# Six modulation chunks of the second layer: products and sums on GpSimd in place of TensorE

## The chip, the cores and the metric

The kernel runs on one core of a Trainium2 chip. The metric is device time in microseconds (us) for one execution; lower is better. Engines are named as the profile names them: PE (TensorE), PEld (TensorE's weight load), DVE (VectorE), ACT (ScalarE), POOL (GpSimd) and SP (SyncE, which here only issues transfers).

## The reference

Two blocks follow one another. The first is a transformer of two layers (256 tokens, width 2048) with three kinds of attention. The second is a block with retention, an mLSTM and a mixture of experts, and its norms are modulated by six rows that come from one vector `c`:

```
sh1, sc1, gt1, sh2, sc2, gt2 = split(silu(c) @ w_ada + b_ada, 6)
csh1, csc1, ... = split(silu(c_ctx) @ w_ada + b_ada, 6)
rq, rk, ... = split_in(modulate(x, norm1_g, sh1, sc1) @ w_in)
crq, ...    = split_in(modulate(ctx, norm1_g, csh1, csc1) @ w_in)
x = x + gt1 * merge(...)
x = x + gt2 * peer(modulate(x, norm2_g, sh2, sc2), ...)
```

`w_ada` is 2048 x 12288. Of the rows for the context only `csh1` and `csc1` are used, since the context isn't updated in the last (here the only) layer.

## The kernel before

All large weights come through one ring of four buffers, `ring`, each 128 x 2048 numbers (1 MB, a "piece"): SP issues one transfer after the other (L882), in the order of the list `RING`, each after a wait on `piece_used` of its buffer. A weight piece is then cut into a high part by ACT (the cast to `high`, L1883) and a low part by DVE (the subtraction `ring_r`, L2506). PE multiplies it in three passes (L300 to L302), 24 matmuls of 512 columns for a piece, and its last matmul counts `piece_used` up, whereupon SP may fill the buffer anew. Inside a layer the pieces have slots 0 to 87; beside the slots PE does the attention's matmuls.

`w_ada` is cut into 24 chunks of 512 columns. Fourteen are done within the two layers: chunk `a` has four pieces that stand in the ring between weight pieces, after the slots of `ADA_SLOTS` (seven chunks for each layer). These modulation pieces are not split. For each, PE runs `ada_pe` (L340): four fp32 matmuls with two stationary columns (silu of `c` and of `c_ctx`) and 512 moving columns, one in each quarter of the array, into PSUM bank 7. After the fourth piece ACT copies the four quarters' rows to `mod_rows` in SBUF (`ada_act`, L359), PE sums them over the quarters and turns them into columns (`ada_turn`, L353), and DVE copies these into `adac` (`ada_dve`, L368). Other work in this stretch that the change stands beside: POOL issues side transfers in a written order (query weights, the residual, context columns, `pT` and `w_ple` for the embedding products at L1245), each after a wait for the slot that frees its place.

Of the kernel before, what the change touches and what calls it, by code (L numbers as in the profile page):

```python
# [26 lines left out]
ALU = mybir.AluOpType  # L27
# [3 lines left out]
P = 128  # L31
# [4 lines left out]
PIECE_KT = 4  # L36
CHUNK = 512
PIECE = PIECE_KT * CHUNK
PIECES = 4
DEPTH = 2  # L40
# [77 lines left out]
C_SILU = C_CONV + 3 * 8  # L118
# [17 lines left out]
ADA_SLOTS = ((3, 5, 7, 9), (12, 14, 16, 18), (28, 30, 32, 34), (38, 40, 42, 44), (59, 61, 63, 65), (68, 70, 72, 74), (77, 79, 81, 83))  # L136
ADA_LAYER = len(ADA_SLOTS)
ADA_L = DEPTH * ADA_LAYER


def layer_order():
# [23 lines left out]
def build_program(nc, t):  # L165
    ctx = ExitStack()
    with ctx:
# [172 lines left out]
        def ada_pe(pe, a, j):  # L340
# [9 lines left out]
                               ring[:, b, q * CHUNK:(q + 1) * CHUNK], start=(j == 0), stop=(j == 3), tile_position=(0, 32 * q))  # L350
            mm.then_inc(piece_used[b], 1)

        def ada_turn(pe, a):  # L353
            pe.wait_ge(ada_rows, a + 1)
            for b in range(4):
                mm = pe.matmul(ps[:, 7, 2 * b:2 * b + 2], mod_rows[:, b * P:(b + 1) * P], sel16[:, 0:2], start=True, stop=True)
            mm.then_inc(ada_turned, 1)
# [9 lines left out]

        def ada_dve(dve, a):  # L368
            dve.wait_ge(ada_turned, a + 1)
            dve.tensor_copy(adac[:, 4 * a:4 * a + 4, :], ps[:, 7, 0:8].rearrange("p (b r) -> p b r", r=2)).then_inc(ada_done, 1)  # L370


# [579 lines left out]
        def _(pool):  # L952
            for n, (name, l) in enumerate(STAGES):
# [8 lines left out]
                elif name == "layers":  # L962
                    for l in range(DEPTH):
                        pool.wait_ge(tile_low, TILES(l, "x", 8))
                        pool.wait_ge(x_square, l + 1)
                        if l >= 1:
                            pool.wait_ge(h_spilled, 16)
                        for k in range(3):
                            if k:
                                b, u, _ = W_AT[l, 2 * k]  # L970
                                pool.wait_ge(piece_used[b], u + 1)
                            pool.dma_start(w_uq[:, k, :], t["w_uq"][l][k * P:(k + 1) * P, :]).then_inc(layer_loads, 16)
                        b, u, _ = W_AT[l, 6]
                        pool.wait_ge(piece_used[b], u + 1)
                        pool.dma_start(w_ukv, t["w_ukv"][l].rearrange("(k p) n -> p k n", p=P)).then_inc(layer_loads, 16)
                        pool.wait_ge(at_out, HEADS * (l + 1))
                        pool.wait_ge(at_done, HEADS * (l + 1))
                        pool.dma_start(hx_of[l], (HRES if l else t["x"]).rearrange("(t p) d -> p t d", p=P)).then_inc(layer_loads, 16)
                        if l + 1 == DEPTH:
                            pool.dma_start(trig[:, :, :, :], t["trig2"]).then_inc(consts_p, 16)  # L980
                            pool.dma_start(b_ada, t["b_ada"]).then_inc(consts_p, 16)
                            for e in range(4):
                                b, u, _ = W_AT[l, (57, 59, 61, 63)[e]]
                                pool.wait_ge(piece_used[b], u + 1)
                                pool.dma_start(crows[:, :, e, :], t["ctx"][:, e * CHUNK:(e + 1) * CHUNK].rearrange("(t p) d -> p t d", p=P)).then_inc(consts_p, 16)
                            pool.wait_ge(tile_full, TILES(l, "mixed", 9))
                            pool.dma_start(final_g, t["final_g"].partition_broadcast(P)).then_inc(aux, 16)
                        b, u, _ = W_AT[l, OUT_SLOT + OUT_PIECES.index((3, 1))]
                        pool.wait_ge(piece_used[b], u + 1)
                        pool.dma_start(pT, t["pT"][l].rearrange("(k p) n -> p k n", p=P)).then_inc(ple_loaded, 16)  # L990
                        for e in range(4):
                            cs = slice(e * CHUNK, (e + 1) * CHUNK)
                            if e:
                                b, u, _ = W_AT[l, (71, 73, 76)[e - 1]]
                                pool.wait_ge(piece_used[b], u + 1)
                                pool.wait_ge(ple_loaded, 80 * l + 16 * (e + 1))
                            pool.dma_start(w_ple[:, :, cs], t["w_ple"][l][:, cs].rearrange("(k p) n -> p k n", p=P)).then_inc(ple_loaded, 16)
                        if l + 1 < DEPTH:
                            pool.wait_ge(gate_used, 4 * (l + 1))
                            pool.dma_start(HRES.rearrange("(t p) d -> p t d", p=P), hx).then_inc(h_spilled, 16)  # L1000
                    for e in range(4):
                        if e == 3:
                            pool.wait_ge(ada_turned, ADA_L)
                            pool.dma_start(wgates, t["wgates"]).then_inc(aux, 16)
                        pool.wait_ge(gate_used, 4 * (DEPTH - 1) + e + 1)
                        pool.dma_start(HX[:, e * CHUNK:(e + 1) * CHUNK].rearrange("(t p) d -> p t d", p=P), hx_1[:, :, e * CHUNK:(e + 1) * CHUNK]).then_inc(h_saved, 16)
# [59 lines left out]
        def _(pe):  # L1066
# [3 lines left out]
            for n, (name, l) in enumerate(STAGES):  # L1070
                begin(pe, n, () if name in FLOWING or name == "peer" else ALL)
                if name == "layers":
# [306 lines left out]
                    for l in range(DEPTH):  # L1379
                        for q in range(SLOTS):  # L1380
                            if l == 0 and q == 3:
                                pe.wait_ge(tile_low, TILES(0, "x", 8))
                            for p, blocks in parts_of(q):
                                products(l, p, blocks)
                            if l == 0 and q < 2:
                                turn_first_x(2 + q)
                            if l:
                                side(l - 1, q + SLOTS)
                            side(l, q)
                            for a0, slots in enumerate(ADA_SLOTS):  # L1390
                                a = ADA_LAYER * l + a0
                                if q in slots:
                                    if q == 28:
                                        pe.wait_ge(rel_made, 6 * (l + 1))
                                    elif q == 59:
                                        pe.wait_ge(tile_low, TILES(l, "mixed", 5))
                                    ada_pe(pe, a, slots.index(q))
                                elif q == slots[-1] + 1:
                                    ada_turn(pe, a)
                elif name == "kv":  # L1400
# [474 lines left out]
        def _(sc):  # L1875
            for n, (name, l) in enumerate(STAGES):
                begin(sc, n, () if name in FLOWING else ALL)
                if name == "layers":
# [133 lines left out]
                    def side(l, q):  # L2012
# [108 lines left out]
                            elif q - 2 in C_TURN_AT:  # L2121
                                high_of_ctx(C_TURN_AT.index(q - 2))
                        for a0, slots in enumerate(ADA_SLOTS):
                            if q == slots[-1] + 2:
                                ada_act(sc, ADA_LAYER * l + a0)

                    sc.activation(rs[:, 90:91], ones[:, 0:1], ACT.Silu)
# [354 lines left out]
        def _(dve):  # L2482
# [12 lines left out]
            for n, (name, l) in enumerate(STAGES):  # L2495
# [5 lines left out]
                elif name == "layers":  # L2501
# [457 lines left out]
                    use_gate(DEPTH - 1, 3)  # L2959
                    split_dve(dve, kv_piece(2), (2,))  # L2960
                    k0, k1 = 2 * KT, 4 * ADA_L
                    dve.tensor_tensor(adac[:, k0:k1, :], adac[:, k0:k1, :], b_ada[:, k0:k1].unsqueeze(2).to_broadcast([P, k1 - k0, 2]), ALU.add)
                    for rows in part_rows:
                        dve.memset(rows, 0.0)
                    dve.wait_ge(x_square, DEPTH + 2)
# [739 lines left out]
```

## Time and profile before

| | |
|---|---|
| median of 3 runs | 3759.24 us (3757.33 to 3761.44) |
| profiled execution | 3757.12 us, of which the span is 3755.6 us |
| PE busy | 3706.6 us, 99% of the span |
| DVE, ACT, POOL busy | 2365.3, 1575.0, 114.8 us |
| second layer with the six chunks | about 705 to 1256 us of the span |

"Busy" is the union of the instruction times of an engine. A row of the timeline gives start and duration in us, the engine, the line of the kernel, and in brackets how long the engine was idle before and what ended that.

### The profile page before, as it was taken

The numbers are of one execution on the slowest core, as the hardware profiler recorded it, in microseconds if no ns is written. First come the engines' busy times: TensorE is split into PE (matmuls) and PEld (weight loads), VectorE is DVE, ScalarE is ACT, GpSimd is POOL, SyncE is SP. The second block draws the span as 40 slices with busy tenths as digits, with TensorE's granted clock in tenths as the row PEclk, the third lists the DMA queues.
The fourth block names the chain that finished last, engine by engine and source line by source line (L and its number), as shares of the span: only waits on it lengthen the run. The fifth ranks groups of instructions, "written<-read, shape, count | busy, mean of one in ns | idle before, by whom it ended". The sixth has DMA issues, their size and how long they took to land.

```text
span 3755.6 us, 48176 instructions
## 1 busy us (share of the span) xinstructions
PE 3706.6 (99%) x20154; PEld 3123.8 (83%) x20154; DVE 2365.3 (63%) x3164; ACT 1575.0 (42%) x1562; POOL 114.8 (3%) x157
## 2 busy tenths in 40 slices
PE   8999999999999999999999999999999999999998
PEld 6777777777777778988888899999988888888886
DVE  4366545347645667565746579777566666667777
ACT  5344544344444522256443433355433333333333
POOL 0000000000000000020000000000000000000000
PEclk9999999999999999999999999999999999999999
DMA  7445565645566467543466445556666666666664
GB/s 274 168 172 202 194 262 198 269 146 191 198 261 241 161 247 283 206 173 134 153 225 246 165 172 187 207 218 229 226 236 235 223 223 223 223 246 235 236 250 175
DMA packets 119530, 799.35 MB, mean 213 GB/s; under 512 B 13424, under 2 KB 13808, under 8 KB 32304
## 3 DMA queue, kind: packets, MB, share of 16 engines
q1 hardware_dynamic: 96992, 692.73, 51.1%
q0 software_dynamic: 20048, 82.96, 5.7%
q10 hardware_dynamic: 2304, 20.97, 1.3%
q8 instruction: 142, 2.33, 0.2%
q14 instruction: 44, 0.36, 0.0%
HBM read 752.57 MB, written 44.04 MB: 212 GB/s over the span
## 4 chain that ended last, share of the span: by engine, by line
PE 93%; DVE 3%; DMA 2%; ACT 1%; POOL 1%; issue 0%; DVEq 0%; SPq 0%; POOLq 0%; ACTq 0%
PE ps L300 25%; PE ps L301 24%; PE ps L302 24%; PE ps L1808 5%; PE ps L1810 2%; DMA ring<-in_stream_dram 2%; PE ps L1760 2%; PE ps L349 1%; PE ps L1245 1%; PE ps L1109 1%; DVE ring_r L2506 1%; PE ps L1599 1%; DVE ring_r L314 1%; PE ps L1076 0%; PE ps L1077 0%; ACT high L1883 0%
## 5 line engine op out<-in xcount | busy, mean ns | idle before, releaser
L308 ACT CAST high<-ring 128x2048 fp32r<-128x2048 f32 x384 | 733.7, 1912 | 1185.0 <-DMA ring<-in_stream_dram 1180.1
L314 DVE TENSOR_TENSOR ring_r<-ring,high 128x2048 fp32r<-128x2048 f32 x384 | 880.4, 2294 | 536.9 <-ACT high L308 534.5
L302 PE MATMUL ps<-high,act_r 128*128 128x512 f32 x1952 | 762.7, 391 | 0.0
L300 PE MATMUL ps<-high,z_r 128*128 128x512 f32 x1728 | 677.8, 392 | 2.7 <-DVE ring_r L2506 2.3
L301 PE MATMUL ps<-ring_r,z_r 128*128 128x512 f32 x1728 | 673.1, 390 | 0.0
L300 PE MATMUL ps<-high,h_r 128*128 128x512 f32 x1600 | 644.9, 403 | 9.5 <-DVE ring_r L2506 5.5
L301 PE MATMUL ps<-ring_r,h_r 128*128 128x512 f32 x1600 | 625.0, 391 | 0.0
L2506 DVE TENSOR_TENSOR ring_r<-ring,high 128x2048 fp32r<-128x2048 f32 x176 | 402.9, 2290 | 348.7 <-ACT high L1883 347.2
L302 PE MATMUL ps<-high,z_r 128*128 128x512 f32 x1376 | 535.9, 389 | 0.0
L301 PE MATMUL ps<-act_r,high 128*128 128x256 f32 x1664 | 471.6, 283 | 0.0
L1883 ACT CAST high<-ring 128x2048 fp32r<-128x2048 f32 x176 | 335.0, 1909 | 252.2 <-DMA ring<-in_stream_dram 251.2
L302 PEld LDWEIGHTS ps<-high,act_r 128*128 128x128 f32 x1952 | 367.3, 188 | 79.3
L300 PE MATMUL ps<-act_r,high 128*128 128x256 f32 x1472 | 420.6, 286 | 2.4 <-DVE act_r L3388 2.4
L302 PE MATMUL ps<-act_r,ring_r 128*128 128x256 f32 x1472 | 417.3, 283 | 0.0
L300 PEld LDWEIGHTS ps<-high,h_r 128*128 128x128 f32 x1600 | 301.2, 188 | 114.9 <-issue 44.9
L300 PEld LDWEIGHTS ps<-high,z_r 128*128 128x128 f32 x1728 | 324.6, 188 | 84.0 <-issue 12.6
L301 PEld LDWEIGHTS ps<-ring_r,z_r 128*128 128x128 f32 x1728 | 324.8, 188 | 66.5 <-issue 0.5
L301 PEld LDWEIGHTS ps<-ring_r,h_r 128*128 128x128 f32 x1600 | 301.6, 189 | 58.3 <-issue 0.7
L301 PEld LDWEIGHTS ps<-act_r,high 128*128 128x128 f32 x1664 | 320.3, 192 | 0.0
L302 PEld LDWEIGHTS ps<-high,z_r 128*128 128x128 f32 x1376 | 258.3, 188 | 54.2
L1808 PE MATMUL ps<-act_r,high 128*128 128x512 f32 x832 | 294.8, 398 | 0.0
L300 PEld LDWEIGHTS ps<-act_r,high 128*128 128x128 f32 x1472 | 283.3, 192 | 2.5 <-issue 2.5
(511 smaller groups left out, 3973.8 us busy)
## 6 DMA issues: line engine op xcount, KB each, us to landing
ring<-in_stream_dram SPq DMA_DIRECT2D x656, 1024.0 KB, 4.8
hidden<-z POOLq DMA_DIRECT2D x32, 512.0 KB, 6.4
gate_matrix<-z ACTq DMA_DIRECT2D x8, 2048.0 KB, 7.2
r<-gate_matrix POOLq DMA_DIRECT2D x32, 512.0 KB, 6.2
z<-hidden POOLq DMA_DIRECT2D x32, 512.0 KB, 6.6
r<-in_w_ple_dram POOLq DMA_DIRECT2D x8, 512.0 KB, 5.8
merge_gates<-r ACTq DMA_DIRECT2D x8, 512.0 KB, 4.8
r<-merge_gates POOLq DMA_DIRECT2D x4, 1024.0 KB, 5.4
```

The source lines that it names most:

```text
L300: pe.matmul(out, lhs[0], rhs[0], start=start, stop=False)
L301: pe.matmul(out, lhs[0], rhs[1], start=False, stop=False)
L302: return pe.matmul(out, lhs[1], rhs[0], start=False, stop=stop)
L308: sc.copy(high[:, j, :], ring[:, j, :]).then_inc(piece_high[j], 1)
L314: dve.tensor_tensor(ring_r[:, j, :], ring[:, j, :], high[:, j, :], ALU.subtract).then_inc(piece_low[j], 1)
L349: mm = pe.matmul(ps[32 * q:32 * q + 2, 7, :], cols[:, C_SILU + 2 * k:C_SILU + 2 * k + 2], ring[:, b, q * CHUNK:(q + 1) * CHUNK], start=(j ...
L1109: mm = pe.matmul(ps[:, bank, (hd % 2) * TOK:(hd % 2 + 1) * TOK], w[:, k, hd * HD:(hd + 1) * HD], src[:, k, :], start=(k == 0), stop=(k == ...
L1760: mm = pe.matmul(ps[:, 4 + t // 4 % 4, (t % 4) * P:(t % 4 + 1) * P], hot1[:, k % HOTS, t % 8, :], hot2[:, k % HOTS, t % 8, :], start=True, ...
L1808: mm = pe.matmul(ps[:, b, :].rearrange("p (s n) -> p s n", s=2), w[0], halves_2(k), start=(k == 0), stop=(k == KT - 1))
L1810: mm = pe.matmul(ps[:, b, TOK:], w[1], high_2(k), start=False, stop=False)
L1883: sc.copy(high[:, b, :], ring[:, b, :]).then_inc(piece_high[b], 1)
L2506: dve.tensor_tensor(ring_r[:, b, :], ring[:, b, :], high[:, b, :], ALU.subtract).then_inc(piece_low[b], 1)
```

## The change

Chunks 8 to 13, all of which belong to the second layer and none of which the context needs, leave PE's matmuls. For each piece of these chunks POOL multiplies each of four 512-column parts by one column of silu(c) (a number for each partition) and adds it to `mod_rows`, in place, one instruction after the other with a semaphore between. POOL frees the ring's buffer when it is through the piece. PE then sums over all 128 partitions: `ada_turn` multiplies `mod_rows` by a column of ones. ACT's copies for these chunks are gone, DVE copies one column where it copied two. The pieces' places in the ring stay. In the diff `chain` is a semaphore count with a wait for it on the same engine.

```diff
+ADA_POOL = (8, 9, 10, 11, 12, 13)
...
+        def ada_pool(pool, a, j):
+            b, u = A_AT[a, j]
+            if j == 0:
+                pool.wait_ge(ada_turned, a)
+            pool.wait_ge(piece_full[b], 16 * (u + 1))
+            for q in range(PIECE_KT):
+                k = PIECE_KT * j + q
+                w, c = ring[:, b, q * CHUNK:(q + 1) * CHUNK], cols[:, C_SILU + 2 * k:C_SILU + 2 * k + 1]
+                if k == 0:
+                    o = pool.tensor_scalar(mod_rows, w, c, None, ALU.mult)
+                else:
+                    chain(pool, "pool", pool.tensor_scalar(w, w, c, None, ALU.mult))
+                    o = pool.tensor_tensor(mod_rows, mod_rows, w, ALU.add)
+                if q < PIECE_KT - 1:
+                    chain(pool, "pool", o)
+            o.then_inc(piece_used[b], 1)
+            pool.wait_ge(piece_used[b], u + 1)
+            if j == 3:
+                pool.drain().then_inc(ada_rows, 1)
...
         def ada_turn(pe, a):
             pe.wait_ge(ada_rows, a + 1)
+            if a in ADA_POOL:
+                pe.wait_ge(ada_done, a)
+                for b in range(4):
+                    mm = pe.matmul(ps[:, 7, 2 * b:2 * b + 1], mod_rows[:, b * P:(b + 1) * P], ones[:, 0:1], start=True, stop=True)
+                mm.then_inc(ada_turned, 1)
+                return
...
                         pool.dma_start(w_ukv, t["w_ukv"][l].rearrange("(k p) n -> p k n", p=P)).then_inc(layer_loads, 16)
+                        if l + 1 == DEPTH:
+                            for a in (8, 9, 10):
+                                for j in range(4):
+                                    ada_pool(pool, a, j)
...
                                 pool.dma_start(crows[:, :, e, :], t["ctx"][:, e * CHUNK:(e + 1) * CHUNK].rearrange("(t p) d -> p t d", p=P)).then_inc(consts_p, 16)
+                                ada_pool(pool, 11, e)
...
+                            ada_pool(pool, 12, 0)
+                            ada_pool(pool, 12, 1)
...
+                                if l + 1 == DEPTH and e < 3:
+                                    ada_pool(pool, 12, e + 1)
+                                elif l + 1 == DEPTH:
+                                    ada_pool(pool, 13, 0)
...
+                    for j in range(1, 4):
+                        ada_pool(pool, 13, j)
...
-                                    ada_pe(pe, a, slots.index(q))
+                                    if a not in ADA_POOL:
+                                        ada_pe(pe, a, slots.index(q))
```

On PE, at the third piece of chunk 11 (slot 63 of the second layer), `ps` is PSUM, `z_r` and `r_r` the left operands in two parts; before:

```order
L300 MATMUL ps<-high,z_r 128x512
L301 MATMUL ps<-ring_r,z_r 128x512
L302 MATMUL ps<-high,z_r 128x512
L349 MATMUL ps<-ring,cols 2x512 [waits piece_full2]
L349 MATMUL ps<-ring,cols 2x512 x3
L300 MATMUL ps<-high,r_r 128x512 [waits piece_low3,evac0]
L301 MATMUL ps<-ring_r,r_r 128x512
```

With the change the two rows of L349 are gone there, and 23 times more; the wait for `piece_low3` follows directly on slot 63's last matmul. On POOL, at the same stretch (the context's columns, the final weights' row, then chunk 12), before:

```order
L981 DMA r<-in_b_ada_dram 128x96
L985 DMA act<-in_ctx_dram 128x2x512 x4
L987 DMA z<-in_final_g_dram 128x2048
L990 DMA r<-in_pT_dram 128x2x256
L997 DMA r<-in_w_ple_dram 128x2x512 x4
```

and with the change, from the second of the four context transfers on, through the second piece of chunk 11 to the third transfer:

```order
L1020 DMA act<-in_ctx_dram 128x2x512
L366 TENSOR_SCALAR ring<-ring,cols 128x512
L367 TENSOR_TENSOR wsmall<-wsmall,ring 128x512
L366 TENSOR_SCALAR ring<-ring,cols 128x512
L367 TENSOR_TENSOR wsmall<-wsmall,ring 128x512
L366 TENSOR_SCALAR ring<-ring,cols 128x512
L367 TENSOR_TENSOR wsmall<-wsmall,ring 128x512
L366 TENSOR_SCALAR ring<-ring,cols 128x512
L367 TENSOR_TENSOR wsmall<-wsmall,ring 128x512
L1020 DMA act<-in_ctx_dram 128x2x512
```

`wsmall` holds `mod_rows`. POOL's queue now holds eight instructions (seven for the first piece of a chunk) between such transfers, each piece behind a wait for its landing.

## Rows read from the trace of the kernel before

**Rows 1.** The page: busy time (share) xinstructions; granted clock by slices, tenths.

```profile
PE 3706.6 (99%) x20154; PEld 3123.8 (83%) x20154; DVE 2365.3 (63%) x3164; ACT 1575.0 (42%) x1562; POOL 114.8 (3%) x157
PEclk9999999999999999999999999999999999999999
```

**Rows 2.** Waits of PEld from 705 to 1256 us: total, times, longest.

```profile
PEld ps L300 <- DVE ring_r L2506: 7.0, 7, 2.1
```

**Rows 3.** Busy time from 705 to 1256 us: all engines; L349 alone; L2506 alone.

```profile
705.00:1256.00 551.00, 547.06 (x2639) 424.09 (x2637) 306.06 (x506) 255.86 (x334) 10.18 (x15) 1.00 0.57 210
705.00:1256.00 551.00, 26.01 (x200) 2.66 (x200) 1.00 0.57 210
705.00:1256.00 551.00, 173.97 (x76) 1.00 0.57 210
```

**Rows 4.** Timeline: third piece of chunk 11, its buffer's next filling, that piece's way.

```profile
1094.62 0.33 SPq L882 DMA_DIRECT2D ring<-in_stream_dram  x1
1106.68 1.04 PE L349 MATMUL ps<-ring,cols 128*2 128x512 f32 x8
1107.78 0.33 SPq L882 DMA_DIRECT2D ring<-in_stream_dram  x1
1118.31 1.91 ACT L1883 CAST high<-ring 128x2048 fp32r<-128x2048 f32 x1 [2.62 <-DMA ring<-in_stream_dram]
1120.25 2.29 DVE L2506 TENSOR_TENSOR ring_r<-ring,high 128x2048 fp32r<-128x2048 f32 x1 [3.73 <-ACT high L1883]
1122.60 0.50 PE L300 MATMUL ps<-high,z_r 128*128 128x512 f32 x1 [1.16 <-DVE ring_r L2506]
```

**Rows 5.** Timeline of SP: issue and next filling, shortest (chunk 12) and longest (chunk 8).

```profile
1154.05 0.33 SPq L882 DMA_DIRECT2D ring<-in_stream_dram  x1
1167.14 0.33 SPq L882 DMA_DIRECT2D ring<-in_stream_dram  x1
743.42 0.33 SPq L882 DMA_DIRECT2D ring<-in_stream_dram  x1
774.62 0.33 SPq L882 DMA_DIRECT2D ring<-in_stream_dram  x1
```

**Rows 6.** The ring's 101 transfers of that stretch.

```profile
DMA to landing us min/median/max: 4.6/4.8/10.5
```

**Rows 7.** Timeline of POOL's twelve sums, first to last, and of DVE beside them.

```profile
1633.44 2.31 POOL L385 TENSOR_TENSOR act<-z,trig 128x512 f32<-128x512 f32 x1
...
1642.31 1.29 POOL L388 TENSOR_TENSOR act<-z,trig 128x512 f32<-128x512 f32 x1
1643.67 1.29 POOL L389 TENSOR_TENSOR z<-act 128x512 f32<-128x512 f32 x1
1644.91 3.36 POOL L390 TENSOR_TENSOR z<-act 128x512 f32<-128x512 f32 x1
...
1656.82 1.26 POOL L390 TENSOR_TENSOR z<-z 128x512 f32<-128x512 f32 x1
1632.30 5.60 DVE L314 TENSOR_TENSOR ring_r<-ring,high 128x2048 fp32r<-128x2048 f32 x2
...
1644.59 2.52 DVE L314 TENSOR_TENSOR ring_r<-ring,high 128x2048 fp32r<-128x2048 f32 x1
```

**Rows 8.** POOL's other one-tensor instructions: count, busy us, mean ns.

```profile
L957 POOL TENSOR_SCALAR_AFFINE_SELECT ident<-ident 128x128 f32<-128x128 f32 x1 | 0.3, 292 | 0.2 <-POOL ident L956 0.2
L960 POOL IOTA iota<- 128x128 f32 x1 | 0.2, 238 | 0.0
L956 POOL MEMSET ident<- 128x128 f32 x1 | 0.2, 205 | 0.3 <-POOLq L3696 0.3
L3696 POOL MEMSET const-float32-0.0<- 128x1 f32 x1 | 0.1, 98 | 0.5 <-issue 0.5
```

**Rows 9.** A side transfer of POOL, and PE's first use of what it brings.

```profile
1148.68 0.72 POOL L997 DMA_DIRECT2D r<-in_w_ple_dram  x1
...
L1245 PE MATMUL ps<-r x32: 590/592/593, 1178.9 to 1249.8; 128*128 128x512 f32 x32
```

More of the change, by code:

```diff
@@ L369, in ada_dve @@
             dve.wait_ge(ada_turned, a + 1)
+            if a in ADA_POOL:
+                dve.tensor_copy(adac[:, 4 * a:4 * a + 4, 0], ps[:, 7, 0:8:2]).then_inc(ada_done, 1)
+                return
             dve.tensor_copy(adac[:, 4 * a:4 * a + 4, :], ps[:, 7, 0:8].rearrange("p (b r) -> p b r", r=2)).then_inc(ada_done, 1)
@@ L2123, in side @@
                         for a0, slots in enumerate(ADA_SLOTS):
-                            if q == slots[-1] + 2:
+                            if q == slots[-1] + 2 and ADA_LAYER * l + a0 not in ADA_POOL:
                                 ada_act(sc, ADA_LAYER * l + a0)
@@ L2961, in _ @@
                     k0, k1 = 2 * KT, 4 * ADA_L
-                    dve.tensor_tensor(adac[:, k0:k1, :], adac[:, k0:k1, :], b_ada[:, k0:k1].unsqueeze(2).to_broadcast([P, k1 - k0, 2]), ALU.add)
+                    dve.tensor_tensor(adac[:, k0:k1, 0], adac[:, k0:k1, 0], b_ada[:, k0:k1], ALU.add)
                     for rows in part_rows:
```

## The prediction, on record before the change was timed

> **What bounds the kernel now.** I read the page first: PE is busy 99% of the span and its granted clock stays in the top tenth throughout [rows 1]; that is the 2.4 GHz level, so no clock effect is to be had. A matmul taken off PE is therefore worth its time, as long as the pieces behind it are ready earlier too. Next I cut out the stretch of the six chunks, 705 to 1256 us: PE busy 547.06 of 551 us, DVE 306.06, POOL only 10.18 [rows 3]. Then the waits: PE's loads waited seven times, 7.0 us in all, for DVE's subtraction of a ring piece [rows 2]. So in seven places the ring and not PE set the pace already. The timeline of one such place shows the chain [rows 4]: the third piece of chunk 11 is issued at 1094.62, PE multiplies it at 1106.68 for 1.04 us, its buffer is filled anew from 1107.78, that transfer lands at 1118.31 (the cast waited for it), cast and subtraction take until 1122.54, and PE, idle for 1.16 us, starts at 1122.60. Whoever frees this buffer 1 us later stops PE 1 us longer.
>
> **Taken away.** L349's rows in the stretch are 200 for 26.01 us, that is 25 pieces (one belongs to chunk 7) of 1.04 us [rows 3]. 24 go: **-25.0 us of PE**. ACT loses 24 copies of small rows and DVE half a column copy; neither was waited for at those places, so 0. `ada_turn` keeps four small matmuls: 0.
>
> **Added: POOL's time for a piece.** Four products and four sums (three for the first piece of a chunk, 3.75 on average). A sum of 128x512 alone takes 1.29 us, and after a semaphore the next starts 0.07 us later [rows 7]. There is no product in the trace. The nearest rows are one-tensor instructions of 128 columns, 205, 238 and 292 ns against 98 ns for one column [rows 8]; stretched to 512 columns they give 0.52, 0.66 and 0.87 us. I take the middle, 0.66; above, 1.29 bounds it (a sum, which reads two tensors). So 4 x 0.66 + 3.75 x 1.29 + 7 x 0.07 = 8.0 us if nothing disturbs.
>
> Something does. Of the twelve sums of 1633 us, those that met DVE's subtraction took 2.31 and 3.36 us, each ending 1.3 us after the subtraction did; the twelve took 24.6 us from first to last in place of 15.5. The subtractions were lengthened too: 5.60 us for two, 2.52 for one, against 2.29 [rows 4, 7]. The two engines shut each other out for whole instructions. The Trainium skill says just this ("SBUF — State Buffer", on what contends): a DVE instruction with two SBUF inputs and a GpSimd one that reads SBUF share a port, and the second to start blocks until the first has ended. By that rule, the trace agrees.
>
> In the stretch the subtractions alone fill 173.97 of 551 us, 32% [rows 3]: 8.0 / 0.68 = 11.8. I take **11.5 us for a piece** (low 7.4, all products at 0.52 and never blocked; high 16.6, products at 1.29 and the 1.6-fold stretching of rows 7). For the product the skill has a figure ("GPSIMD Engine Reference", performance versus the Vector engine): 0.77 us for 512 elements in a good loop. By it a piece would take an estimated 12 us and the sum below would be some 5 us worse.
>
> **Where it lands.** What counts is when the buffer is freed. Before, a piece stayed in its buffer from issue to the next filling between 13.1 us and 31.2 us (the first two rows and the last two of [rows 5]). POOL needs 4.8 us for the landing [rows 6] plus 11.5: 16.3. I went through all 24: ten stay less than 16.3 us now (three pieces each of chunks 9 and 12, three of 11, one of 10; 13.0 to 15.7, together 144.5), and these are freed later, by 18.5 us together: **+18.5**. The other fourteen are freed at the same time or earlier, which the next pieces hardly need. With 9.5 us for a piece it is three pieces and 2.9 us, with 14 us fifteen pieces and 46.6 us: this term is steep, and the forecast hangs on it.
>
> **DVE behind POOL.** POOL is busy 24 x 11.5 = 276 us, half of the stretch. Half of the 76 subtractions meet it and wait about 0.5 us (0.23 and 1.0 shown, [rows 7]): 19 us, of which PE feels what finds no slack. A third, I choose, since about a quarter of the weight pieces are ready under 1.2 us before PE takes them and the attention's DVE steps run into POOL as well: **+6**. Bounds 0 and 19.
>
> **Ring already late.** At seven places PE waited for the chain [rows 2]; the microsecond saved before them is worth something only if the chain moves too. Seven times half of 1.04: **+3.5** (0 to 7).
>
> **Moved on POOL's queue.** The transfers behind the sums: `pT` and the first `w_ple` go out at 1148.68 and are wanted at 1178.9 [rows 9]. With the second piece of chunk 12 ahead of them (issued 1141, landed 1146, 11.5 us) they go out at about 1158, so 20 us of cover is left; a POOL piece of over 20 us would spend it. The residual's saves after chunk 13 have no reader near. Cost 0. PE's turn of a chunk comes one slot after its last piece, about 7 us behind PE's old use of it, and 14 us or more behind the landing in every chunk: 0.
>
> Sum: -25.0 + 18.5 + 6 + 3.5 = **+3.0 us**. The profiled execution took 3757.12 us, which gives 3760; it lies 2.1 below the median of the runs shown, so against that median 3762. I say **3761 us**. A measurement of this kernel tells about 0.2% (7.5 us) from no change.
>
> **Rivals.**
> 1. *The sums fit.* A piece on POOL takes about 9.5 us: products at 0.52 to 0.6, and POOL slips between the subtractions. For it: POOL was idle for 540 of 551 us. Against it: the blocking of rows 7. Then -25.0 + 2.9 + 5 + 3.5 = -14, 3743 to 3750. Chance 0.27.
> 2. *POOL is the ring's slowest user.* A product costs nearer 1 us or more, or small DVE steps with two inputs each let one POOL instruction pass: 14 us a piece. Then -25.0 + 46.6, less what slack of up to 4 us for a piece takes (about half of it, 15 pieces x 1.5), + 8 + 3.5 = +10, and with 16 us some +30: 3767 to 3790. Its place is the index and selection part (chunk 9) and the output slots (chunks 11, 12), and it decides from about 12.5 us a piece. Chance 0.31.
> 3. *No effect at all*, since PE waits for the ring in place of multiplying; it lies in the forecast's range.
>
> The forecast, losses and gains nearly even (3752 to 3766), has 0.42. From these cases: faster 0.28, same 0.40, slower 0.32. Eight in ten: 3744 to 3780; the likeliest case alone 3753 to 3767.
>
> **What the profile after would show.** L349 with 256 rows in place of 448; POOL busy about 280 us more; one product 0.6 to 0.9 us; sums of 1.3 us alone and 2.3 to 3.4 beside a subtraction; subtractions above 2.29 on average; PE's waits for L2506 risen from 7 us to 25 or 30 in the stretch, after the pieces of chunks 9, 11 and 12. I am wrong if a piece takes under 10 us or over 13, if the waits of PE come from POOL's turn (`ada_rows`) or the embedding's weights, or if DVE's attention steps and not the ring stop PE.

## The result and the profile after: 0.7% slower

The changed kernel takes 3783.47 us (median of 4 runs, 3782.11 to 3787.58) where the kernel before takes 3759.45 (3757.33 to 3761.44) on the same chip: a ratio of 1.0068, 95% interval 1.0056 to 1.0080, some 25 us slower. The forecast was 3761 with a range to 3780: the time lies above the range. The profiled execution spans 3786.0 us, against 3755.6 before.

The page after, engines and granted clock (before: [rows 1]), and the first line of the chain that ended last:

```profile
PE 3698.7 (98%) x19962; PEld 3132.3 (83%) x19962; DVE 2408.6 (64%) x3164; ACT 1561.0 (41%) x1538; POOL 468.3 (12%) x343
PEclk9999999999999999999999999999999999999999
PE 86%; POOL 6%; DVE 3%; DMA 3%; ACT 1%; issue 1%; DVEq 0%; POOLq 0%; SPq 0%; ACTq 0%
```

POOL's share of the chain rose from 1% to 6%. It was taken to be busy 280 us longer; it is 354. PE has 25 us less to multiply, yet its busy time fell by only 7.9 us.

POOL's groups from 705 to 1290 us (L366 and L364 are products, L367 sums):

```profile
L366 POOL TENSOR_SCALAR ring<-ring,cols 128x512 f32<-128x512 f32 x90 | 197.6, 2196 | 33.7 <-DMA ring<-in_stream_dram 25.8
L367 POOL TENSOR_TENSOR wsmall<-wsmall,ring 128x512 f32<-128x512 f32 x90 | 141.4, 1571 | 7.5
L364 POOL TENSOR_SCALAR wsmall<-ring,cols 128x512 f32<-128x512 f32 x6 | 13.7, 2284 | 101.1 <-DMA ring<-in_stream_dram 101.1
```

The timeline of the first piece of chunk 9 on POOL:

```profile
848.29 1.57 POOL L364 TENSOR_SCALAR wsmall<-ring,cols 128x512 f32<-128x512 f32 x1 [61.36 <-DMA ring<-in_stream_dram]
849.95 3.13 POOL L366 TENSOR_SCALAR ring<-ring,cols 128x512 f32<-128x512 f32 x1
853.17 1.28 POOL L367 TENSOR_TENSOR wsmall<-wsmall,ring 128x512 f32<-128x512 f32 x1
854.55 1.57 POOL L366 TENSOR_SCALAR ring<-ring,cols 128x512 f32<-128x512 f32 x1
856.20 1.30 POOL L367 TENSOR_TENSOR wsmall<-wsmall,ring 128x512 f32<-128x512 f32 x1
857.59 3.48 POOL L366 TENSOR_SCALAR ring<-ring,cols 128x512 f32<-128x512 f32 x1
861.16 1.30 POOL L367 TENSOR_TENSOR wsmall<-wsmall,ring 128x512 f32<-128x512 f32 x1
```

An undisturbed product takes 1.57 us, more than a sum, and a disturbed one 3.13 and 3.48. This piece takes 14.2 us from its first start to its last end; over all 24, read off the timeline in the same way, it is 12.6 to 18.2, on average 15.3. Since a piece that lands while POOL is at another one waits up to 7.3 us more, the mean from landing to release is 17.3 us; it was 13.3 before.

Who waited: PE from 700 us and SP from 640 us, both to 1310 (total, times, longest). The first row is PE's wait for DVE's subtraction of a weight piece, the second its wait for POOL's sums at its turn, the third SP's wait for a buffer that POOL holds:

```profile
PE ps L301 <- DVE ring_r L2551: 36.1, 18, 6.9
PE ps L380 <- POOLq L373: 5.4, 3, 2.6
...
SPq L913 <- POOL wsmall L367: 152.5, 20, 14.4
```

Before, PE's waits for the subtraction were 3.9 us in the same stretch. SP waited 20 times with the next load for POOL's last sum.

Two different delays stand in the 36.1 us. A piece can land late, because POOL freed its buffer late. Or it lands in time, and DVE subtracts late or slowly, because its own steps stand behind POOL's reads. For each of PE's 18 waits the timelines tell how much later the subtraction began than its cast ended and how much longer than 2.29 us it ran; PE's wait, as far as this lateness covers it, adds up to 13.1 us (0.6 of 3.9 before). The other 23 us are late landings, among them nearly all of the two longest waits (4.37 and 6.86 us, ahead of slots 66 and 73). A wait of 2.56 us at 880 us is mostly of the second kind (2.0 us of it): its piece landed at 874.38, the cast ended at 876.32, but DVE was still in a group of short two-input steps. Cast, DVE's last steps and subtraction there, and at the end the same two steps before:

```profile
874.41 1.91 ACT L1928 CAST high<-ring 128x2048 fp32r<-128x2048 f32 x1 [8.63 <-DMA ring<-in_stream_dram]
876.39 1.31 DVE L420 TENSOR_TENSOR z<-r 128x160 f32<-128x160 f32 x1
877.62 0.31 DVE L421 TENSOR_TENSOR z<-r 128x160 f32<-128x160 f32 x1
877.97 2.67 DVE L2551 TENSOR_TENSOR ring_r<-ring,high 128x2048 fp32r<-128x2048 f32 x1
...
880.43 0.33 DVE L389 TENSOR_TENSOR z<-r 128x160 f32<-128x160 f32 x1
880.67 0.32 DVE L390 TENSOR_TENSOR z<-r 128x160 f32<-128x160 f32 x1
```

The prediction did not foresee what the stalls do next. Windows of 2 us around this one (PE busy stands first, the granted clock third from the end), and PE's matmuls there:

```profile
876.00:878.00 2.00, 2.00 (x10) 1.43 (x8) 1.93 (x4) 1.48 (x2) 1.90 (x2) 1.00 0.10 41
878.00:880.00 2.00, 0.12 (x1) 0.00 (x0) 2.00 (x1) 0.74 (x1) 1.92 (x2) 1.00 0.33 61
880.00:882.00 2.00, 1.31 (x4) 1.07 (x5) 1.93 (x8) 0.00 (x0) 1.90 (x2) 0.76 0.98 410
882.00:884.00 2.00, 2.00 (x6) 1.53 (x5) 1.93 (x7) 0.00 (x0) 1.92 (x2) 0.50 0.13 53
884.00:886.00 2.00, 2.00 (x9) 1.63 (x8) 1.71 (x1) 0.00 (x0) 2.00 (x1) 0.89 0.00 0
```

```profile
877.51 0.39 PE L302 MATMUL ps<-ring_r,h_r 128*128 128x512 f32 x1
877.73 0.39 PE L303 MATMUL ps<-high,act_r 128*128 128x512 f32 x1
880.69 0.54 PE L301 MATMUL ps<-high,h_r 128*128 128x512 f32 x1 [2.56 <-DVE ring_r L2551]
...
881.45 0.63 PE L303 MATMUL ps<-high,act_r 128*128 128x512 f32 x1
881.88 0.63 PE L301 MATMUL ps<-high,h_r 128*128 128x512 f32 x1
```

After 2.56 us of idle PE the granted clock is 0.50, the 1.2 GHz level, and the matmuls follow at 0.43 us where it had been 0.22. So part of the stall is paid a second time, here 1.7 us (the sum of (1 - clock) x 2 over these windows). (The Trainium skill says that PE's clock is gated by how busy it has been recently: "TensorE: Matmul & The Clock Gate", Part 1. By that, the trace agrees.) In windows of 10 us from 700 to 1310, the sum of (1 - clock) x 10 is 13.6 us after and 0.0 before. Outside this stretch, up to PE's last matmuls, it is 12.0 us after and 6.9 before; one of the falls after, at 686 us, stands ahead of POOL's first piece (720), so such falls also come without POOL's work. On the page's forty slices such falls are too short to show.

The loss can be added up from the two traces: -25.0 (matmuls gone) + 37.6 (PE's waits, 36.1 + 5.4 - 3.9) + 13.6 (clock) = +26.2, against 30.4 between the two spans. Some 4 us are not assigned; the 5.1 us of clock outside the stretch are as large, and no run shows that the change causes them.

### The profile page after: what moved, and what is told of

The parts are those of the page before. It is cut to its first block, busy times and chain, and to the rows that moved or that the text cites. A ratio compares the mean times of both kernels' runs of the same rounds, so it can differ in the third digit from the quotient of the medians.

```text
span 3786.0 us, 47976 instructions
## 1 busy us (share of the span) xinstructions
PE 3698.7 (98%) x19962; PEld 3132.3 (83%) x19962; DVE 2408.6 (64%) x3164; ACT 1561.0 (41%) x1538; POOL 468.3 (12%) x343
## 3 DMA queue, kind: packets, MB, share of 16 engines
q8 instruction: 140, 2.29, 0.2%
## 4 chain that ended last, share of the span: by engine, by line
PE 86%; POOL 6%; DVE 3%; DMA 3%; ACT 1%; issue 1%; DVEq 0%; POOLq 0%; SPq 0%; ACTq 0%
PE ps L301 23%; PE ps L303 23%; PE ps L302 23%; PE ps L1853 5%; POOL ring L366 3%; DMA ring<-in_stream_dram 3%; PE ps L1855 2%; POOL wsmall L367 2%; PE ps L1805 2%; PE ps L350 1%; DVE ring_r L2551 1%; PE ps L1153 1%; PE ps L1644 1%; DVE z L3079 1%; DVE ring_r L315 0%
## 5 line engine op out<-in xcount | busy, mean ns | idle before, releaser
L315 DVE TENSOR_TENSOR ring_r<-ring,high 128x2048 fp32r<-128x2048 f32 x384 | 879.8, 2292 | 540.7 <-ACT high L309 538.3
L2551 DVE TENSOR_TENSOR ring_r<-ring,high 128x2048 fp32r<-128x2048 f32 x176 | 420.4, 2389 | 345.8 <-ACT high L1928 344.2
```

The source lines that it names most:

```text
L315: dve.tensor_tensor(ring_r[:, j, :], ring[:, j, :], high[:, j, :], ALU.subtract).then_inc(piece_low[j], 1)
L2551: dve.tensor_tensor(ring_r[:, b, :], ring[:, b, :], high[:, b, :], ALU.subtract).then_inc(piece_low[b], 1)
```

## Experiments

Times are medians. The kernel before, in the runs' company, took 3756.4 to 3758.3 us.

**1. The products left out** (`w` itself is summed; of 96 products the six that begin a chunk stay, so the result is wrong).

```diff
-                    chain(pool, "pool", pool.tensor_scalar(w, w, c, None, ALU.mult))
```

> Leaves out the products: POOL only adds the four parts of a piece to mod_rows, so the modulation rows are wrong. Theory A (a piece's time on POOL decides, by when its buffer is freed): a piece takes 4 sums of 1.3 us plus blocking, 7 to 8 us, and is freed before PE used to free it; most of the 25 us taken off PE is kept, 3738 to 3748 us. Theory B (the shared port decides, by what it does to DVE's subtractions and small steps): POOL still reads SBUF for some 180 us of the stretch, half of the 350 us of the changed kernel, so about half of the loss stays, 3765 to 3773 us.

3744.19 us, ratio 0.9970 (0.9959 to 0.9981), in A's band. A piece takes 6.8 us on POOL on average (5.4 to 9.7). With a short piece the change gains; no wait of SP for POOL is left in the view of waits, and PE waits 11.5 us. All the same, by its ratio only 11 of the 25 us arrive.

**2. The product as a two-tensor instruction**, all else equal.

```diff
+                cb = c.to_broadcast([P, CHUNK])
...
-                    chain(pool, "pool", pool.tensor_scalar(w, w, c, None, ALU.mult))
+                    chain(pool, "pool", pool.tensor_tensor(w, w, cb, ALU.mult))
```

> The same result, with the product written as a two-tensor multiplication, the silu column being read as a broadcast, in place of the product with a pointer scalar that took 1.57 us alone. Theory A: a product takes 1.3 us like a sum, a piece 1.1 us less (about 14.3 us); ten to twenty pieces are freed late now, so 8 to 15 us come back, 3768 to 3775 us. Theory B: POOL holds the port nearly as long, 3780 to 3784 us. If the broadcast is slow to read, the product takes 1.57 us or more and the time is that of the changed kernel or above.

3774.62 us, ratio 1.0045 (1.0028 to 1.0062), in A's band: about 9 us come back. The same multiplication takes 1.42 us on average in place of 2.20, and 1.04 undisturbed in place of 1.57 (group, and duration min/median/max of the line):

```profile
L367 POOL TENSOR_TENSOR ring<-ring,cols 128x512 f32<-128x512 f32 x90 | 127.5, 1416 | 68.8 <-DMA ring<-in_stream_dram 62.8
...
L367 POOL TENSOR_TENSOR ring<-ring,cols x90: 1038/1042/3158, 723.2 to 1262.1; 128x512 f32<-128x512 f32 x90
```

SP's waits for POOL fall from 152.5 to 83.6 us, and a piece takes 12.7 us (10.1 to 16.1) in place of 15.3. PE's waits fall less, to 30.7 us for the subtraction and 2.3 us for another step of DVE, and 15.9 of the 30.7 are DVE's lateness. The longest, 6.11 us, is nearly all of that kind. Its piece landed at 875.26 and was cast by 877.20, while DVE went through a group of six short steps, two of them shown here; each took 1.06 to 1.54 us in place of 0.32 to 0.45 and ended 0.2 to 0.3 us after a POOL instruction did. The last row shows the multiplication of L418 in the kernel before:

```profile
876.40 1.54 DVE L418 TENSOR_TENSOR r<-z,trig 128x160 f32<-128x160 f32 x1
881.61 1.42 DVE L422 TENSOR_TENSOR z<-r 128x160 f32<-128x160 f32 x1
883.07 2.29 DVE L2552 TENSOR_TENSOR ring_r<-ring,high 128x2048 fp32r<-128x2048 f32 x1
885.41 0.80 PE L301 MATMUL ps<-high,h_r 128*128 128x512 f32 x1 [6.11 <-DVE ring_r L2552]
...
879.25 0.43 DVE L386 TENSOR_TENSOR r<-z,trig 128x160 f32<-128x160 f32 x1
```

**3. The port alone.** PE keeps its matmuls and frees the buffers; POOL runs as many instructions of the same kinds on `mod_rows` alone, the sum being a subtraction of the tile from itself, which takes 1.04 us in place of 1.29 (the six chunks' result is not computed).

```diff
-                w, c = ring[:, b, q * CHUNK:(q + 1) * CHUNK], cols[:, C_SILU + 2 * k:C_SILU + 2 * k + 1]
+                w, c = mod_rows, cols[:, C_SILU + 2 * k:C_SILU + 2 * k + 1]
...
-                    o = pool.tensor_tensor(mod_rows, mod_rows, w, ALU.add)
...
-            o.then_inc(piece_used[b], 1)
-            pool.wait_ge(piece_used[b], u + 1)
+                    o = pool.tensor_tensor(mod_rows, mod_rows, w, ALU.subtract)
...
-                                    if a not in ADA_POOL:
-                                        ada_pe(pe, a, slots.index(q))
+                                    ada_pe(pe, a, slots.index(q))
```

> PE keeps its matmuls for the 24 pieces and frees their buffers as before; POOL runs the same eight instructions for each piece, at the same places, but on mod_rows alone (the rows that result are zeros, so the output is wrong), and does not hold a buffer. Only the shared port is left of the change, and 25 us of PE are not saved. Theory A: the port costs 5 to 12 us over the kernel before, 3764 to 3771 us. Theory B: the port costs what the change lost, the 24 us measured plus the 25 us saved on PE, 3795 to 3810 us.

3776.47 us, ratio 1.0052 (1.0036 to 1.0069), between the two theories. PE's waits from 700 to 1310 show why it isn't the pure price of the port:

```profile
PE ps L377 <- POOLq L370: 13.3, 3, 6.1
PE ps L301 <- DVE ring_r L2547: 2.5, 4, 1.0
```

13.3 us are PE standing at its turn for POOL's sums, and 8.5 us are clock after that; PE's waits for the ring are no longer than before. This run does not price the port by itself, and it shows that late sums on POOL can stop PE directly. In the changed kernel that wait was 5.4 us.

**4. The late release alone.** POOL reads no SBUF: 28 chained memsets hold each piece (the six chunks' result is not computed).

```diff
+HOLD = 6
...
-                    chain(pool, "pool", pool.tensor_scalar(w, w, c, None, ALU.mult))
-                    o = pool.tensor_tensor(mod_rows, mod_rows, w, ALU.add)
+                for _ in range(HOLD):
+                    chain(pool, "pool", pool.memset(mod_rows, 0.0))
+                o = pool.memset(mod_rows, 0.0)
```

> POOL holds each of the 24 pieces for 28 chained writes of zeros to mod_rows (0.5 us each by the row of a 128-column write stretched, so 14 to 16 us a piece) and reads nothing from SBUF; the rows are zeros, so the output is wrong. Theory A: late buffers alone make most of the loss, 3770 to 3785 us. Theory B: without reads the port is free, the 25 us saved on PE are kept, 3738 to 3748 us.

3787.70 us, ratio 1.0086 (1.0069 to 1.0103), above A's band. From its first memset (719.58) to the end of its last (736.11) POOL takes 16.5 us for the first piece, 16.4 on average, longer than in the changed kernel (15.3); with the queue, landing to release is 19.6 us on average where it is 17.3 there. DVE's subtractions met no reader and stayed at their old length, yet PE waited as in the changed kernel:

```profile
L2550 DVE TENSOR_TENSOR ring_r<-ring,high 128x2048 fp32r<-128x2048 f32 x76 | 174.0, 2290 | 168.5 <-ACT high L1927 167.8
PE ps L302 <- DVE ring_r L2550: 41.4, 16, 5.9
```

Late buffers alone can make a loss as large as the whole one, but these buffers are later than the changed kernel's, so this run does not say that they make all of its loss. Only 0.7 of the 41.4 us are DVE's lateness.

**5, 6, 7. The same with 24, 20 and no memsets** (in the last, one column is written and the buffer freed).

> Held buffers alone with 24 chained memsets a piece, about 14 us (20 of them, 11.7 us, gave 3737.8; 28 of them, 16.3 us, gave 3787.7). Output not computed for the six chunks. Theory A (the time rises ever more steeply with the hold: buffers that come free later stall PE, and stalls take the clock down): 3748 to 3762, less than half way, with the clock between 0.993 and 0.996. Theory B (a step where the first pieces queue behind one another, near 13 us): 3765 or more.

> As in the run that only held the buffers, but with 20 chained memsets a piece in place of 28, so that GpSimd holds a piece for 20 x (0.53 + 0.05) = about 11.7 us after its landing, which is what my prediction took for the whole product and sum (11.5 us). It reads no SBUF, so DVE's subtractions should stay at 2.29 us. Output not computed for the six chunks. Theory A (the prediction's sum was right but for the time of a piece): -25.0 + 20 (buffers freed later) + 3.5 (ring late already), no cost at DVE: -1.5 us, 3752 to 3762 against 3758. Theory B (the loss comes with any use of GpSimd here: its queue, the turn that PE waits for, pieces that queue behind one another): 3768 us or more.

> GpSimd writes one column of its sums at each piece's landing and frees the buffer; no product, no sum, output not computed for the six chunks. It is the most that taking the matmuls off PE can give. Theory A (PE's 25.0 us are worth their time when the buffers come free early): -25.0 + 0 to 3.5 us where the ring is late already, 3733 to 3740 us. Rival C (the ring's loads have their own pace, DMA and cast, and PE would wait for them in place of multiplying): 3745 to 3752 us, with PE's waits for the subtraction above 20 us in the stretch of the six chunks.

The four points (a piece's time on POOL; clock lost as above, 700 to 1310; PE's waits for the subtraction there, 3.9 before; sums and spans against the kernel before):

| POOL holds a piece | time, ratio | PE waits | clock lost | -25.0 + both | span |
|---|---|---|---|---|---|
| at once | 3731.51, 0.9938 (0.9923 to 0.9954) | 6.2 | 0.0 | -22.7 | -27.3 |
| 11.7 us | 3737.83, 0.9954 (0.9938 to 0.9969) | 9.2 | 1.7 | -18.0 | -21.0 |
| 14 us | 3753.37, 0.9990 (0.9981 to 1.0000) | 20.7 | 3.4 | -4.8 | -5.4 |
| 16.5 us | 3787.70, 1.0086 (1.0069 to 1.0103) | 41.4 + 0.8 | 20.5 | +33.8 | +29.6 |

By the ratios (times 3757) holding each piece 11.7 us costs 6 us in all against freeing it at once, the next 2.3 us cost 13.5 more, the last 2.5 us 36. At 11.7 us the result lies 14 us below the lower of the two theories' bands (A: 3752 to 3762); freed at once, it is 1.5 us below A's band, so rival C, a ring with its own pace, falls; at 14 us it is in A's. The bend is partly the clock's.

Beside them stand the kernels whose POOL reads the pieces (the mean time of a piece and from landing to release, read off the timelines in the same way; "behind DVE" is the part of PE's waits that DVE's lateness covers):

| | piece, landing to release | ratio | PE waits | behind DVE | clock lost | -25.0 + both | span |
|---|---|---|---|---|---|---|---|
| run 1 | 6.8, 7.0 us | 0.9970 | 11.5 | 4.6 | 1.7 | -15.7 | -15.0 |
| run 2 | 12.7, 13.6 us | 1.0045 | 30.7 + 2.3 | 15.9 | 15.3 | +19.4 | +19.0 |
| the change | 15.3, 17.3 us | 1.0068 | 36.1 + 5.4 | 13.1 | 13.6 | +26.2 | +30.4 |
| held 14 us | 14.1, 15.0 us | 0.9990 | 20.7 | 0.7 | 3.4 | -4.8 | -5.4 |
| held 16.5 us | 16.4, 19.6 us | 1.0086 | 41.4 + 0.8 | 0.7 | 20.5 | +33.8 | +29.6 |

Run 2 holds its pieces for less time than the run held for 14 us and is 0.55% (some 20 us) slower. So the time of the hold is not the whole cause: POOL's reads delay DVE as well. A straight line between the held runs gives an estimate of 15 us of loss at the changed kernel's 15.3 us; measured are some 25, so about 10 us come from the reads. By the same working run 2 has some 28 us from them and run 1 some 8. The split is an estimate, since the holds are uneven and the ring's slack is shared between the two delays. That the clock is a real term shows in the last two columns: without it run 2 would be off by 15 us, and run 3 (13.3 + 2.5 - 3.9 + 8.5 = 20.4, spans 20.2 apart) by 8.

**8. Chunk 8 alone on POOL**, the one with long stays before.

```diff
-ADA_POOL = (8, 9, 10, 11, 12, 13)
+ADA_POOL = (8,)
```

> Only the first of the six chunks on GpSimd, the one whose pieces stayed 13.6, 16.1, 26.3 and 17.5 us in their buffers before (from landing to release) and 13.4, 14.9, 17.0 and 15.1 us with the change; the other five on PE as before. Theory A (the hold of a piece decides): the gain of 4.2 us that the change shows at the end of this chunk stays to the end: 3752 to 3756 against 3758, ratio 0.9985 to 0.9995. Theory B (the port's cost decides, also where the hold does not): no gain, 3758 to 3762.

**9. The same with the two-tensor product.**

> The same, with the product as a two-tensor instruction whose second operand is the broadcast column (about 1.3 us in place of 1.57 undisturbed). Theory A: a piece takes about 1 us less, the hold was short enough already: 3751 to 3755, at most 1 us better than the run with chunk 8 alone. Theory B: as that run, 3757 to 3761.

**10. Chunks 8, 10 and 13, two-tensor product.**

> Chunks 8, 10 and 13 on GpSimd with the broadcast product, those whose first pieces stayed 13.6 to 20.5 us in their buffers before; 9, 11 and 12 on PE as before. 12 pieces leave PE: -12.5 us. Theory A (hold decides): a piece takes about 14.5 us disturbed; the holds before were 13.6 to 26.3 (chunk 8), 18.8, 13.9, 12.7, 10.6 (chunk 10), 19.8, 12.1, 13.6, 12.4 (chunk 13): freed later by 0.6, 1.8, 3.9 and 2.4, 0.9, 2.1 us, together 11.7, half of it felt, and port 3: -12.5 + 6 + 3 = -3.5: 3750 to 3757. Theory B (every piece on GpSimd loses): 3760 or more.

3753.47 (ratio 0.9994, 0.9985 to 1.0003), 3754.21 (0.9992, 0.9983 to 1.0001) and 3755.45 (0.9996, 0.9987 to 1.0005): all three in A's bands of time, none distinguishable from the kernel before. They speak against a loss with every piece and show no gain; the two theories of the first two lie too close for this measurement. In the third PE waits 8.3 us for the subtraction, and 6.4 of them are DVE's lateness.

**11. PE kept busy in its stalls.** The changed kernel with eight small matmuls ahead of eight slots whose piece was late.

```diff
+FILL = (31, 34, 63, 66, 71, 73, 80, 82)
...
+                            if l == 1 and q in FILL:
+                                for _ in range(8):
+                                    pe.matmul(ps[0:2, 7, 64:192], ones[:, 0:2], ident[:, :], start=True, stop=True)
```

> The changed kernel, with eight small matmuls (ones by identity, 128 columns, into columns of bank 7 that nobody reads; some 1.7 us in all) on PE just before each of the eight places where its trace shows PE idle for 1.85 to 6.86 us for a ring piece (start of slots 31, 34, 63, 66, 71, 73, 80, 82 of the second layer). They add 13.6 us of PE work and nothing else. The trace of the changed kernel shows the granted clock at the 1.2 GHz level after such idle times (six stretches of some 3.4 us each between 880 and 1290 us, mean clock 0.992 against 0.997 before). Theory A (part of the loss is the clock: 10 to 15 us of it): some of these falls go, the clock returns to 0.994 or more, and the time is 3770 to 3781. Theory B (the loss is idle time alone, the clock costs nothing): the fillers hide in the idle time at best: 3783 to 3797, no less.

3782.55 us (3778.41 to 3785.67), ratio 1.0066 (1.0051 to 1.0081): neither theory's band, and no different from the changed kernel. PE's waits for the ring fell from 36.1 to 23.7 us and the clock's loss from 13.6 to 8.5. The 64 matmuls were busy for 15.3 us:

```profile
L1428 PE MATMUL ps<-ident,ones 128*2 128x128 f32 x128 | 15.3, 272 | 0.0
```

The fillers stand for the most part in time in which PE was idle, and what they won back (12.4 us of waits, 5.1 of clock) is about what they cost. That the clock's share is worth its 13.6 us is read from the granted clock and the matmuls' intervals; this run does not show it.

**12. The products on ACT.** All six chunks, complete. ACT multiplies each 512-column part in place in the ring, after its own steps of the slot; POOL waits for each part and only sums; the first sum of a chunk takes two parts at once.

```diff
+        def ada_products(sc, a, j):
+            b, u = A_AT[a, j]
+            sc.wait_ge(piece_full[b], 16 * (u + 1))
+            for q in range(PIECE_KT):
+                k = PIECE_KT * j + q
+                w = ring[:, b, q * CHUNK:(q + 1) * CHUNK]
+                sc.activation(w, w, ACT.Copy, scale=cols[:, C_SILU + 2 * k:C_SILU + 2 * k + 1]).then_inc(ada_made, 1)
...
+                pool.wait_ge(ada_made, 16 * ADA_POOL.index(a) + k + 1)
+                if k == 0:
+                    continue
+                if k == 1:
+                    o = pool.tensor_tensor(mod_rows, ring[:, b, 0:CHUNK], w, ALU.add)
```

> All six chunks, complete: the products are made on ACT in place in the ring (activation with the column as its scale, after ACT's steps of the slot), GpSimd waits for each and only sums (15 sums a chunk). An ACT instruction of 128x512 takes 0.58 to 0.69 us in the changed kernel's trace, so a piece costs ACT some 2.6 us, 62 us in all where ACT was busy for 364 of 585 us. GpSimd's part is that of the run with the products left out (3744.2), begun some 0.7 us later. Theory A (the time from landing to release decides, and a piece that takes about as long as in that run gives its gain): 3744 to 3751, ratio 0.996 to 0.9985. Theory B (what GpSimd's work moves from PE is given back on the next engine: ACT's casts come later, ACT is the ring's slowest user): 3757 or more, with PE waiting for subtractions that waited for casts.

3745.14 us (3741.33 to 3747.73), ratio 0.9967 (0.9955 to 0.9979), in A's band: 13 us faster than the kernel before and some 38 faster than the change. Timeline of the first piece of chunk 11, on ACT and POOL:

```profile
1092.08 2.56 ACT L384 ACTIVATE ring<-ring,cols 128x512 f32<-128x512 f32 x4 [0.94 <-DMA ring<-in_stream_dram]
1092.90 5.84 POOL L369 TENSOR_TENSOR wsmall<-wsmall,ring 128x512 f32<-128x512 f32 x4 [4.46 <-ACT ring L384]
```

6.7 us from first product to last sum; POOL's part takes 6.1 us on average. In the views of waits from 640 and 700 us, and in the group of DVE's subtractions:

```profile
SPq L924 <- POOL wsmall L369: 6.4, 4, 2.8
PE ps L302 <- DVE ring_r L2565: 13.1, 12, 2.4
L2565 DVE TENSOR_TENSOR ring_r<-ring,high 128x2048 fp32r<-128x2048 f32 x78 | 184.5, 2365 | 106.3 <-ACT high L1939 105.3
```

ACT's 61.6 us of products find their room in its waits for landings (705 to 1290 us): the casts' are 53.0 us and the products' 41.3, where the casts' were 143.9 in the changed kernel and 100.9 before. Of PE's 13.1 us, 4.9 are DVE's lateness. The sum closes: -25.0 + (13.1 - 3.9) + 3.4 (clock) = -12.4, and the spans differ by -12.6.

## Why the prediction was wrong, step by step

- **What bounds the kernel**: PE, with the ring close behind. Right. The sentence that "no clock effect is to be had" was wrong: it looked only for a gain. A clock at its upper level can be lost, and 13.6 us were.
- **Taken away, -25.0**: right in size (the line's matmuls, L350 now, fell to 256). Freed at once, 23 us of it arrive.
- **POOL's time for a piece, 11.5 us, low 7.4, high 16.6**: the step that failed. Of its terms the sum (1.29) was right, the mutual blocking right in kind (it stretched 11.6 us to 15.3, by 1.32, where 1 / 0.68 is 1.47), the product was not: 0.66 us, stretched from small one-tensor instructions [rows 8], measured at 1.57. Even the upper bound, 1.29, lay under it. Four products add 3.6 us undisturbed. The stated 11.5 is also 0.3 below the 11.8 of its own working, without a reason. With 1.57 that working gives 4 x 1.57 + 3.75 x 1.29 + 0.49 = 11.6, over 0.68 that is 17.1, on the far side of the measured 15.3. The Trainium skill's 0.77 us for 512 elements in a good loop ("GPSIMD Engine Reference", performance versus the Vector engine) is half of the 1.57 measured here; the measurement decides.
- **Where it lands, +18.5 for 11.5 us**: the second error, and in the other direction. This term and the +3.5 for the late ring made 22; the run that held each piece for 11.7 us without reading SBUF lost some 8 of the 25 us. A microsecond of later release was counted as a microsecond of PE, but pieces with slack absorb it at first. For 14 us the working has +46.6 and +3.5; the run held for 14 us lost 21 of the 25. From there to 16.4 us the held runs lose 36 us more, about what the working would count (15 late pieces, 2.4 us each), though a good part of it is other than counted: pieces queue behind one another on POOL (up to 7.3 us in the changed kernel, left out of the working), and the clock falls. So the slope came out about right, in part by luck, and its start was too early.
- **DVE behind POOL, +6**: right in kind, too small, and not on the subtractions alone. Their mean rose from 2290 to 2517 ns, but DVE's other two-input steps were delayed too, and subtractions stood behind them: 13.1 us of PE's waits, within the stated 0 to 19. With the clock's falls, the comparison with the held runs puts the reads at about 10 us in the changed kernel and 28 in run 2 (estimates). Where PE had no late buffers and stood 13.3 us at its turn, in run 3, its waits for the ring did not rise (2.5 us).
- **Ring already late, +3.5**: the run freed at once shows 2.3 us more waiting and by its ratio 1.7 us of the 25 missing, half to two thirds of it.
- **Moved on POOL's queue, 0; PE's turn, 0**: the embedding's weights stopped nothing. The turn did: PE waited 5.4 us for POOL's sums, which the prediction excluded because the turn came 14 us or more behind the landing; landing to the last sum is 17.3 us on average and up to 24.0.
- **The rivals**: rival 2 (the product at 1 us or more, 14 to 16 us a piece, 3767 to 3790) is what happened; its place (chunks 9, 11, 12) fits too, since PE's longest stalls, 4.37 and 6.86 us, are ahead of slots 66 and 73. So does its remark that small DVE steps each let one POOL instruction pass: run 2's six steps show it. Its turning point, 12.5 us, is too early for a hold alone (the line through the held runs crosses zero near 14.3 us) and not too early with POOL's reads: run 2, with 12.7 us, loses. It should have been the likeliest: the only full-size row of a POOL instruction [rows 7] was nearer to the product than the small ones were.

## What to carry to other kernels

Before work moves to an idle engine inside a ring, compare that engine's time for a piece, with its blocked instructions and its queue, to the time that the buffer can stay occupied: in the held runs the move earned most of what it took away up to 11.7 us a piece, and above 14 us the loss grew steeply. Then ask what the engine's own reads do to its neighbour: where POOL read the pieces, even 6 to 7 us a piece (runs 1 and 12) brought only 11 to 14 of the 25 us. Price an operation that the trace lacks by the row of the same size on the same engine, and let the bounds go above it. Split such work so that each engine has only what it does quickly: with the products on ACT and the sums on POOL the same change gains 0.33% in place of losing 0.7%.

## What the hardware showed that I had not expected

- On POOL a 128x512 multiplication by one number for each partition takes 1.57 us as a tensor-scalar instruction and 1.04 us as a tensor-tensor instruction with that column broadcast; the sum of two tiles takes 1.28 to 1.30, a subtraction of a tile from itself 1.04 (run 3), a memset of the same size 0.53. On ACT four such products take 2.56 us.
- POOL instructions that only write SBUF leave DVE's two-input subtractions alone: 2290 ns on average beside 672 memsets, against 2517 beside products and sums. The Trainium skill says so ("SBUF — State Buffer", who interferes with whom: such a DVE instruction contends with a GpSimd one that reads SBUF, not with one that only writes it); by that, the trace agrees.
- Short two-input steps of DVE each stood behind one POOL instruction that reads SBUF: 128x160 multiplications of 0.43 to 0.45 us took 1.18 to 1.54 us in run 2, and PE stood still for 6.11 us though its piece had long landed.
- One idle time of 2.56 us on PE was followed by matmuls at the 1.2 GHz level (0.43 us apart where 0.22 before), in a kernel whose page shows the highest clock in all forty slices.
